# A two-layer hybrid decoder step on one core: first loads in pieces, first unit in halves, squares behind the operands, norm of FFN 1 a unit later

## The reference

```python
h = x + 0.5 * SwiGLU_1(RMSNorm(x))
u = RMSNorm(h)
p = u @ w_in            # attention q, k, v; delta q, k, v, z, beta, alpha; two gates
A = sliding_window_attention(q, k, v, sinks) @ w_attn_o
B = gated_delta_rule(conv(q, k, v), z, beta, alpha) @ w_dn_o
h = h + (sigmoid(gate_a) * A + sigmoid(gate_d) * B) @ w_out
y = h + 0.5 * SwiGLU_2(RMSNorm(h))

def rms_norm(x, w):
    return x * lax.rsqrt(mean(x * x, axis=-1) + EPS) * w
def swiglu_ffn(x, w_gate_up, w_down):
    g, u = split(x @ w_gate_up, 2)
    return (silu(g) * u) @ w_down
```

## Time and profile before

| | |
|---|---|
| median of three runs | 1413.7 us |
| the profiled execution | 1413.78 us |
| its span | 1412.0 us |
| PE busy | 1362.3 us, 96% of the span |
| DVE, ACT, POOL busy | 66%, 41%, 7% |
| share of the chain that ended last | PE 70%, issue 16%, DVE 7% |
| TensorE's clock, mean granted | 0.967 |

### The profile page before, as it was taken

The page is one execution under the profiler, slowest core; times in us unless marked ns, Lnnn a source line. Parts: engine busy times, 40 slices in busy tenths (PEclk is TensorE's granted clock), DMA queues, the critical chain, the costliest instruction groups (busy, mean ns, idle before and its releaser), DMA issues.

```text
span 1412.0 us, 28121 instructions
## 1 busy us (share of the span) xinstructions
PE 1362.3 (96%) x10640; PEld 1322.1 (94%) x10640; DVE 930.4 (66%) x1615; ACT 583.6 (41%) x781; POOL 99.8 (7%) x83
## 2 busy tenths in 40 slices
PE   6999999899999999999989999989999999899999
PEld 6999998899998889999989999988998998899999
DVE  6777558863556957776557775587626568577765
ACT  3444444331343535443435444433313444444444
POOL 3000001230001000000000000012300010000000
PEclk9999999997989999999999999999969999999999
DMA  8554553631222544555535445536212335355454
GB/s 335 184 178 178 209 188 140 97 120 62 91 90 98 204 154 151 179 181 214 198 138 196 178 178 204 212 120 124 71 55 90 107 126 194 120 201 185 179 182 176
DMA packets 42275, 222.01 MB, mean 157 GB/s; under 512 B 13072, under 2 KB 14384, under 8 KB 16688
## 3 DMA queue, kind: packets, MB, share of 16 engines
q1 hardware_dynamic: 29232, 206.91, 40.5%
q10 hardware_dynamic: 12832, 11.92, 3.9%
q0 software_dynamic: 128, 2.08, 0.3%
HBM read 214.48 MB, written 8.49 MB: 158 GB/s over the span
## 4 chain that ended last, share of the span: by engine, by line
PE 70%; issue 16%; DVE 7%; POOL 3%; ACT 2%; DMA 1%; ACTq 0%; DVEq 0%; POOLq 0%; SPq 0%
PE bank L322 21%; PE bank L323 20%; PE bank L324 20%; DVE wlo L303 2%; PE bank L1626 1%; ACT whi L298 1%; POOL rkq L860 1%; DMA out_convs<-cst 1%; PE bank L987 1%; PE bank L906 1%; PE bank L972 1%; PE bank L1539 1%; DVE cv L787 1%; POOL pb__116 L800 1%; DVE x L376 1%
## 5 line engine op out<-in xcount | busy, mean ns | idle before, releaser
L322 PE MATMUL bank<-xh,whi 128*128 128x264 f32 x2032 | 610.6, 301 | 26.9 <-DVE xl L2281 11.0
L323 PE MATMUL bank<-xl,whi 128*128 128x264 f32 x2032 | 587.3, 289 | 0.0
L324 PE MATMUL bank<-xh,wlo 128*128 128x264 f32 x2032 | 586.8, 289 | 0.0
L303 DVE TENSOR_TENSOR wlo<-raw,whi 128x2048 fp32r<-128x2048 f32 (+2 forms) x248 | 441.0, 1778 | 51.1 <-ACT whi L298 45.4
L322 PEld LDWEIGHTS bank<-xh,whi 128*128 128x128 f32 x2032 | 393.5, 194 | 38.0 <-DVE xl L2281 13.9
L298 ACT CAST whi<-raw 128x2048 fp32r<-128x2048 f32 (+2 forms) x192 | 357.2, 1862 | 92.8 <-PE bank L324 73.1
L323 PEld LDWEIGHTS bank<-xl,whi 128*128 128x128 f32 x2032 | 394.8, 194 | 0.2
L324 PEld LDWEIGHTS bank<-xh,wlo 128*128 128x128 f32 x2032 | 392.8, 193 | 0.0
L324 PE MATMUL bank<-hh,wlo 128*128 128x264 f32 x704 | 200.3, 284 | 0.0
L322 PE MATMUL bank<-hh,whi 128*128 128x264 f32 x704 | 199.9, 284 | 0.0
L323 PE MATMUL bank<-hl,whi 128*128 128x264 f32 x704 | 199.6, 283 | 0.0
(11 more groups left out here) (375 smaller groups left out, 1545.2 us busy)
## 6 DMA issues: line engine op xcount, KB each, us to landing
raw<-stream SPq DMA_DIRECT2D x194, 1024.0 KB, 4.8
states<-states ACTq DMA_DIRECT2D x4, 1024.0 KB, 5.3
out_dns<-states ACTq DMA_DIRECT2D x8, 512.0 KB, 2.7
x<-xT SPq DMA_DIRECT2D x2, 528.0 KB, 6.3
con<-consts SPq DMA_DIRECT2D x1, 1049.0 KB, 10.4
kc<-kct ACTq DMA_DIRECT2D x2, 512.0 KB, 6.3
vc<-vct ACTq DMA_DIRECT2D x2, 512.0 KB, 7.0
out_ks<-kcache POOLq DMA_DIRECT2D x2, 508.0 KB, 4.1
```

The lines of the kernel that those rows point to most:

```text
L303: return nc.vector.tensor_tensor(slot(wlo, r, lo, hi), slot(raw, r, lo, hi), slot(whi, r, lo, hi).bitcast(F32), ALU.subtract)
L322: nc.tensor.matmul(out, wh, mh, start=start, stop=False)
L323: nc.tensor.matmul(out, wh, ml, start=False, stop=False)
L324: return nc.tensor.matmul(out, wl, mh, start=False, stop=stop)
```

## The change

On SP, unit 0 is loaded in two halves (gate, up) and x in four quarters, in the order parameters, quarter of x, gate half, three quarters, up half. ACT makes two operands, casts the gate half, makes the other six, casts the up half, casts unit 1, and then makes the squares, which POOL made before. DVE follows it: two `xl`, the gate half of the split, six `xl`, the up half, unit 1's split, and only then the eight sums. PE may start unit 0 with its gate half; for the same unit of the next layer the split is also written as two halves. Sums and spread of n = 0 move: sums behind the gate half of unit 1, spread behind its up half, in both layers. `dve_factor` loses `meanwhile`: the split stands ahead of it, in all three norms. POOL's four cache copies wait for the end of unit 0. ACT's three loads of a layer (`act_loads`) move behind the gate and up units of FFN 1.

```diff
-            split_tail(L, u, r, 0, n).then_inc(w_tail.sem, 1)
+            if isinstance(u, int) and u == UNITS:
+                split_tail(L, u, r, 0, KT).then_inc(w_gate0.sem, 1)
+                split_tail(L, u, r, KT, UT).then_inc(w_tail.sem, 1)
+            else:
+                split_tail(L, u, r, 0, n).then_inc(w_tail.sem, 1)
...
-        def dve_factor(L, n, meanwhile=lambda: None):
+        def dve_factor(L, n):
             nc.vector.wait_ge(ss_ready.sem, ss_ready.at(L, n + 1))
...
             nc.vector.memset(acc[:, :], 0.0).then_inc(acc_clear.sem, 1)
-            meanwhile()
             nc.vector.wait_ge(rstd_ready.sem, rstd_ready.at(L, n + 1))
...
+            sums_at, spread_at = ((1, "gate"), (1, "up")) if ph == 0 else ((0, "gate"), (1, "gate"))
...
-                wait_unit(L, u0 + f)
+                if first and ph == 0:
+                    nc.tensor.wait_ge(w_gate0.sem, w_gate0.at(L, 1))
+                else:
+                    wait_unit(L, u0 + f)
...
-                if first:
+                if isinstance(f, int) and (f, "gate") == sums_at:
                     pe_sums(L, n)
-                if second:
+                if isinstance(f, int) and (f, "gate") == spread_at:
                     pe_spread(L, n)
+                if first and ph == 0:
+                    wait_unit(L, u0)
...
+                if isinstance(f, int) and (f, "up") == spread_at:
+                    pe_spread(L, n)
...
                 if first:
-                    dve_factor(L, n, split)
+                    split()
+                    dve_factor(L, n)
                     dve_spread(L, n)
...
-            dve_factor(L, 1, lambda: split_whole(L, U_BA + AHEAD, (U_BA + AHEAD) % RING))
+            split_whole(L, U_BA + AHEAD, (U_BA + AHEAD) % RING)
+            dve_factor(L, 1)
...
-            load(0, 0, None)
             sp.dma_start(par_all[:, :], params).then_inc(par_in, 16)
-            half = KT // 2 * N
-            for n in range(2):
-                sp.dma_start(x[:, n * half:(n + 1) * half], xT[:, n * half:(n + 1) * half]).then_inc(x_in[n], 16)
+            load_x(0)
+            sp.dma_start(slot(raw, 0, 0, KT), stream[0][:, 0:KT * P]).then_inc(w_first, 16)
+            for n in range(1, 4):
+                load_x(n)
+            sp.dma_start(slot(raw, 0, KT, UT), stream[0][:, KT * P:UT * P]).then_inc(w_loaded[0], 16)
...
-                nc.gpsimd.tensor_tensor(tile_of(sq, m % 2), tile_of(x, m), tile_of(x, m), ALU.mult).then_inc(sq_done.sem, 1)
+            pool.wait_ge(w_used.sem, 2)
...
+            operand(0)
+            operand(1)
+            act.wait_ge(w_first, 16)
+            nc.scalar.copy(slot(whi, 0, 0, KT), slot(raw, 0, 0, KT)).then_inc(head_first, 1)
+            for m in range(2, KT):
+                operand(m)
+            act.wait_ge(w_loaded[0], 16)
+            nc.scalar.copy(slot(whi, 0, KT, UT), slot(raw, 0, KT, UT)).then_inc(w_head.sem, 1)
             act.wait_ge(w_loaded[1], 16)
             nc.scalar.copy(slot(whi, 1), slot(raw, 1)).then_inc(w_head.sem, 1)
+            for m in range(KT):
+                if m >= 2:
+                    act.wait_ge(acc_done.sem, m - 1)
+                nc.scalar.activation(tile_of(sq, m % 2), tile_of(x, m), ACT.Square).then_inc(sq_done.sem, 1)
             with act.Fori(0, DEPTH) as L:
-                act_loads(L)
                 act.wait_ge(par_ready.sem, par_ready.at(L, 1))
                 act_gate_up(L, 0)
+                act_loads(L)
...
+            low(0)
+            low(1)
+            dve.wait_ge(head_first, 1)
+            nc.vector.tensor_tensor(slot(wlo, 0, 0, KT), slot(raw, 0, 0, KT), slot(whi, 0, 0, KT).bitcast(F32),
+                                    ALU.subtract).then_inc(w_gate0.sem, 1)
+            for m in range(2, KT):
+                low(m)
+            split_tail(0, 0, 0, KT, UT).then_inc(w_tail.sem, 1)
+            split_whole(0, 1, 1)
```

More of the change, by code:

```diff
@@ L261, in build @@
         w_tail = sig("w_tail", UNITS)
+        w_gate0 = sig("w_gate0", 1)
         w_used = sig("w_used", UNITS, 1)
@@ L265, in build @@
         ones_in = ctx.enter_context(nc.semaphore("ones_in"))
-        x_in = [ctx.enter_context(nc.semaphore(f"x_in{n}")) for n in range(2)]
+        x_in = [ctx.enter_context(nc.semaphore(f"x_in{n}")) for n in range(4)]
+        w_first = ctx.enter_context(nc.semaphore("w_first"))
+        head_first = ctx.enter_context(nc.semaphore("head_first"))
         ready0 = ctx.enter_context(nc.semaphore("ready0"))
@@ L400, in pe_gate_up, with unit @@
             u0, n = (U_G1, U_G2)[ph], (0, 2)[ph]
-            def unit(f, j, r, first=False, second=False):
+            sums_at, spread_at = ((1, "gate"), (1, "up")) if ph == 0 else ((0, "gate"), (1, "gate"))
+            def unit(f, j, r):
+                first = isinstance(f, int) and f == 0
                 bg, bu = banks[2 * j], banks[2 * j + 1]
-                wait_unit(L, u0 + f)
+                if first and ph == 0:
+                    nc.tensor.wait_ge(w_gate0.sem, w_gate0.at(L, 1))
+                else:
+                    wait_unit(L, u0 + f)
                 nc.tensor.wait_ge(glu_free.sem, glu_free.at(L, ph * FT + f + 1 - RING))
@@ L417, in unit @@
                 mm.then_inc(w_used.sem, 1)
-            unit(0, 1, u0 % RING, True)
+                if isinstance(f, int) and (f, "up") == spread_at:
+                    pe_spread(L, n)
+            unit(0, 1, u0 % RING)
             for j in range(RING):
-                unit(1 + j, (2 + j) % RING, (u0 + 1 + j) % RING, second=j == 0)
+                unit(1 + j, (2 + j) % RING, (u0 + 1 + j) % RING)
             with nc.tensor.Fori(1, FT // RING) as i:
@@ L2185, in load, with load_x @@
                 sp.dma_start(raw[:, r * UT * P:(r + 1) * UT * P], src).then_inc(w_loaded[r], 16)
-            load(0, 0, None)
+            part = KT // 4 * N
+            def load_x(n):
+                sp.dma_start(x[:, n * part:(n + 1) * part], xT[:, n * part:(n + 1) * part]).then_inc(x_in[n], 16)
             sp.dma_start(par_all[:, :], params).then_inc(par_in, 16)
-            half = KT // 2 * N
-            for n in range(2):
-                sp.dma_start(x[:, n * half:(n + 1) * half], xT[:, n * half:(n + 1) * half]).then_inc(x_in[n], 16)
+            load_x(0)
[3 more added lines that the diff above has]
+            sp.dma_start(slot(raw, 0, KT, UT), stream[0][:, KT * P:UT * P]).then_inc(w_loaded[0], 16)
             sp.dma_start(con[:, 0:K_LE], consts[:, 0:K_LE]).then_inc(ones_in, 16)
@@ L2228, in _, with operand @@
         def _(act):
-            act.wait_ge(w_loaded[0], 16)
-            nc.scalar.copy(slot(whi, 0), slot(raw, 0)).then_inc(w_head.sem, 1)
             act.wait_ge(par_in, 16)
-            for m in range(KT):
-                if m % (KT // 2) == 0:
-                    act.wait_ge(x_in[m // (KT // 2)], 16)
+            def operand(m):
+                if m % 2 == 0:
+                    act.wait_ge(x_in[m // 2], 16)
                 nc.scalar.activation(tile_of(xh, m), tile_of(x, m), ACT.Copy,
                                      scale=par_all[:, C_N1 + m:C_N1 + m + 1]).then_inc(xh_done.sem, 1)
+            operand(0)
[6 more added lines that the diff above has]
+            nc.scalar.copy(slot(whi, 0, KT, UT), slot(raw, 0, KT, UT)).then_inc(w_head.sem, 1)
             act.wait_ge(w_loaded[1], 16)
             nc.scalar.copy(slot(whi, 1), slot(raw, 1)).then_inc(w_head.sem, 1)
+            for m in range(KT):
+                if m >= 2:
+                    act.wait_ge(acc_done.sem, m - 1)
+                nc.scalar.activation(tile_of(sq, m % 2), tile_of(x, m), ACT.Square).then_inc(sq_done.sem, 1)
             with act.Fori(0, DEPTH) as L:
-                act_loads(L)
                 act.wait_ge(par_ready.sem, par_ready.at(L, 1))
                 act_gate_up(L, 0)
+                act_loads(L)
                 act_down(L, 0)
@@ L2273, in _, with low @@
             nc.vector.sem_inc(x_done.sem, KT)
-            split_whole(0, 0, 0)
             dve.wait_ge(par_in, 16)
[L2276 to L2279, removed]
+            def low(m):
+                if m % 2 == 0:
+                    dve.wait_ge(x_in[m // 2], 16)
                 dve.wait_ge(xh_done.sem, m + 1)
@@ L2283, in _ @@
                                                op1=ALU.subtract).then_inc(xl_done.sem, 1)
+            low(0)
[7 more added lines that the diff above has]
+            split_whole(0, 1, 1)
+            dve.wait_ge(acc_clear.sem, 1)
+            for m in range(KT):
                 if m:
@@ L2287, in _ @@
                 nc.vector.tensor_tensor(acc[:, :], acc[:, :], tile_of(sq, m % 2), ALU.add).then_inc(acc_done.sem, 1)
-            split_whole(0, 1, 1)
             dve.wait_ge(ones_in, 16)
```

## The result

The changed kernel takes 1418.5 us (median of 8 runs, 1413.9 to 1427.2), the kernel before 1414.7 beside it (8 runs, 1406.4 to 1418.2). The ratio of the runs, which is not the quotient of the two medians (they differ by 3.8 us), is 1.0044 with a 95% interval of 1.0024 to 1.0064: slower by some 6 us, where the prediction had 2.1 and called it no change. Two later comparisons, on two chips, gave 1.0052 (1.0026 to 1.0078) and 1.0058 (1.0034 to 1.0082).

The account below looks back on a forecast made before the run. The prediction took FFN 1's unit 3, waiting on the chain from the norm's spread, as the bound. From 1413.8 us it summed -2.4 (layer 0 start), +3.0 (layer 1) and +1.5 (clock) to 1415.9, range 1412.0 to 1420.5.

Parts of the forecast that it names:

- What bounds the kernel: FFN 1: PE waits for unit 3's low weight part, 10.2 us after the spread starts, through in-order DVE and ACT work.
- The start of layer 0, -2.4: Layer 0: unit 1's load lands at 11.72 as before, spread starts at 26.3 against 28.71, unit 3 2.4 us earlier.
- The rival of late pieces: Layer 0 start: three more SP issues delay unit 1's load by 0 to 5.4 us, giving up to 1421.3; chance 0.08.
- The clock: Clock falls after layer 1's 3.4 us wait, +1.5 us; at layer 0's unit 3 taken as 0, possibly up to 1.5.
- That case: A second clock fall in layer 0, and one in layer 1's mix: 1417.4 to 1418.9 us; chance 0.17.
- the second wait shrinks: Layer 0: a clock fall after the spread's wait slows unit 2, so the wait at unit 3 falls to about 2 us.
- FFN 1 of layer 1, +3.0 and +1.5: Layer 1: spread and unit 3 come 3.0 us later, PE waits about 3.4 us, and the clock falling behind costs 1.5.
- Mix, FFN 2 and the power: Norms of mix and FFN 2: power takes 0.88 us without a split beside it, and the reordering costs nothing there.
- the first rival: All norms: the power stays at 3.06 us, delaying layer 0, layer 1 and mix, giving 1422.6 us; chance 0.08.
- The same: Whole kernel: time within about 0.5% (7 us) of before, between 1406.6 and 1420.8 us; chance 0.87.

Follow-up runs that it names:

- Two later comparisons: The unmodified changed kernel run again beside the kernel before: 1421.8 us against 1414.1, and 1418.3 against 1409.0.
- all four traces: Profiled executions of the changed kernel: the one of the result and three repeats, nothing altered; FFN 1 together 5.2 us longer than in two traces of the kernel before.
- the first trace: The profiled execution of the changed kernel that belongs to the result, 1413.9 us, the least of its eight runs.
- the norm alone: Kernel before plus the split ahead of the factor and FFN 1's sums and spread a unit later, old start: 1416.9 us against 1409.7, ratio 1.0053.
- the second trace: The changed kernel repeated unaltered and profiled; median 1421.8 us where the kernel before took 1414.1, ratio 1.0052.
- The split ahead alone: Kernel before with only the split moved ahead of the factor: 1411.2 us against 1414.1, ratio 0.9969.
- the norm back: Changed kernel with FFN 1's sums and spread again behind the gate halves of units 0 and 1: 1415.6 us against 1409.7 before, ratio 1.0049.

## Why the prediction was wrong

**What bounds the kernel: right.** The place that counted was unit 3, some 10.2 us after the spread: it took 10.33 or 10.34 in layer 0 and 10.23 or 10.24 in layer 1, in all four traces.

**The start of layer 0, -2.4: the step that failed first.** Its premise, that unit 1's load has "the same bytes ahead of it" and so lands at 11.72, doesn't hold: the bytes are the same, but while the gate half loads they move at some two thirds of the rate. The cast came at 13.33. The same slow half put the first matmul at 9.22 (9.2 to 9.5 in the four traces) and not before 8.5, which alone costs nothing, as PE still waits 2.47 us ahead of the spread. Behind the cast the chain was right to 0.2 us in sum, sums of squares (3.88 for 4.0), split, power and `diag` included. The term measured -0.84 in the first trace, -0.5 over all. The rival of late pieces had the right place, with a price of 0 to 5.4; it went to 1.6, by the rate and not by the issues that I had named.

**The clock: the second step.** "I take 0 and keep 1.5 for the range" for a fall at unit 3 in layer 0; it costs 1.7 in the mean, up to 2.7. That case stood among the rivals, with a second one in mix, at 0.17. The spread's wait and unit 3's wait are one chain: where no fall followed the first, unit 2 ran fast and the second wait was the whole 3.3 us. The fall came there in two of the changed kernel's traces; with the norm alone it didn't come, so a wait of this length doesn't settle it. That the second wait shrinks was right for two of four, and in one of these the fall came all the same.

**FFN 1 of layer 1, +3.0 and +1.5: right.** Measured +2.4 and +1.55; the wait is 3.3 for 3.4. The 0.6 is chance at the layer's start: where half clock lasted as long behind the first matmul as before (5.5 us, the second trace; 5.4 and 5.1 before) the term was 3.0, and in the others it lasted 3.4 to 4.4.

The sum of the terms should have been -0.5 + 1.7 + 2.4 + 1.55 = +5.2 instead of +2.1. What the ratios have above 5.2 is in no term that the traces show.

**Mix, FFN 2 and the power: right.** Six powers of 0.85 to 0.88 us, and no wait of PE at the spread of mix. The split ahead alone gives the same six. So the long power was the neighbouring split, and the first rival is out. The Trainium skill (SBUF — State Buffer, section "Who interferes with whom") says of the shared port pair that the two block each other and that the first to issue holds it. The lengths agree with the first half. With the second most don't: in the two traces of the kernel before the power starts 0.13 us ahead of a split ten times, and takes 3.06 us in seven of them and 0.85 in three.

**The chances.** "The same" had 0.87, with 1418.5 inside the range; but a difference of 0.44% was clear of its interval, and the two steps that failed lay both on the side of slower.

## What to carry to other kernels

Find the in-order chain that ends in the wait, here from the norm's spread over two SwiGLUs and a cast to the next unit, and cut it there; moving what stands ahead of it in one place only moves the wait. A wait of some 3 us can cost more than itself, where the clock falls behind it; here it did so in most executions and not in all, so read it from several traces. A transfer cut in pieces for an earlier start may be slower as a whole, as the gate half was here, and make what is queued behind it late.

## What was not expected of the hardware

While the gate half of a unit was loading, the DMA engines were as busy as ever (0.93 to 1.07) at 238 to 256 GB/s; with the whole unit they reached 418 in the same place, and the up half, of the same size and rows, came at full rate a few us later (159 ns a packet against 283). Behind one and the same wait of 3.3 us, half clock lasted 3.4 us in layer 1 and 5.7 to 6.0 in two executions of layer 0, and with the norm alone there was none in layer 0. And with the norm back, an order in POOL's queue cost PE 1.68 us: the cache copies (1.28 and 1.03) wait for the end of unit 0 and stand ahead of the power, so a late unit 0 made the norm late.
